# A two-block sequence model on one core: GpSimd's remainder of each weight block in four instructions of 256 columns instead of one of 1024

## The reference

```python
def swiglu(h, w_gate, w_up, w_down):
    return (jax.nn.silu(h @ w_gate) * (h @ w_up)) @ w_down

for i in range(DEPTH):
    x = x + 0.5 * swiglu(rmsnorm(x, ffn1_norm[i]), ffn1_w_gate[i], ffn1_w_up[i], ffn1_w_down[i])
    h = rmsnorm(x, mix_norm[i]) @ w_in[i]
    ...
    x = x + y @ w_out[i]
    x = x + 0.5 * swiglu(rmsnorm(x, ffn2_norm[i]), ffn2_w_gate[i], ffn2_w_up[i], ffn2_w_down[i])
```

## Time and profile before

| what | us |
|---|---|
| median of 3 runs | 3364.13 (3363.9 to 3365.0) |
| span of the profiled execution | 3360.4 |
| TensorE busy | 3228.2 (96%) |
| VectorE busy | 1812.3 (54%) |
| GpSimd busy | 1835.2 (55%) |
| ScalarE busy | 748.6 (22%) |

### The profile page before, as it was taken

How to read it: one execution, slowest core, us unless ns; L and a number is a source line. 1 busy time by engine, 2 the same in 40 slices (tenths; PEclk the granted TensorE clock), 3 DMA queues, 4 the chain that set the end, 5 groups by cost and what they waited for, 6 DMA issues and landing times.

```text
span 3360.4 us, 44069 instructions
## 1 busy us (share of the span) xinstructions
PE 3228.2 (96%) x14534; PEld 2578.4 (77%) x14534; DVE 1812.3 (54%) x1971; ACT 748.6 (22%) x1260; POOL 1835.2 (55%) x1026
## 2 busy tenths in 40 slices
PE   8999998899999999999889999999999999999998
PEld 6788875578888778876567888788777877888886
DVE  7661277663313765138754331586768886753312
ACT  2110126422201111014532220111122322222200
POOL 5556651066666656663036666644455455666665
PEclk9999999999999999999999999999999999999999
DMA  4222320022323322331012222322122222223322
GB/s 155 81 86 96 113 76 26 9 86 94 100 94 103 110 79 89 100 107 56 13 44 88 98 96 98 118 76 69 63 85 69 76 69 70 94 94 94 97 96 81
DMA packets 77430, 281.26 MB, mean 84 GB/s; under 512 B 9382, under 2 KB 9766, under 8 KB 76776
## 3 DMA queue, kind: packets, MB, share of 16 engines
q1 hardware_dynamic: 74016, 268.58, 24.5%
q10 hardware_dynamic: 3272, 10.79, 0.9%
HBM read 277.24 MB, written 2.10 MB: 83 GB/s over the span
## 4 chain that ended last, share of the span: by engine, by line
PE 79%; DVE 15%; issue 4%; ACT 2%; DVEq 0%; DMA 0%; ACTq 0%; SPq 0%
PE bank L505 24%; PE bank L510 23%; PE bank L509 23%; DVE short L1938 1%; PE bank L640 1%; PE bank L725 1%; PE bank L790 1%; DVE square_sum L1727 1%; DVE xbc L2276 1%; DVE y L1970 1%; DVE x_lo L1717 1%; DVE scaled L2114 1%; PE bank L799 1%; DVE att_qk L2212 0%; DVE reach L2369 0%
## 5 line engine op out<-in xcount | busy, mean ns | idle before, releaser
L451 POOL TENSOR_SCALAR w_hi<-raw 128x1024 fp32r<-128x1024 f32 x504 | 554.8, 1101 | 1451.4 <-PE bank L505 1443.0
L454 POOL TENSOR_TENSOR w_lo<-raw,w_hi 128x1024 fp32r<-128x1024 f32 x504 | 1267.5, 2515 | 42.0
L505 PE MATMUL bank<-x_hi,w_hi 128*128 128x512 f32 x2896 | 1151.3, 398 | 47.7 <-DVE x_lo L1717 21.6
L510 PE MATMUL bank<-x_hi,w_lo 128*128 128x512 f32 x2896 | 1134.6, 392 | 0.0
L509 PE MATMUL bank<-x_lo,w_hi 128*128 128x512 f32 x2896 | 1134.0, 392 | 0.0
L505 PEld LDWEIGHTS bank<-x_hi,w_hi 128*128 128x128 f32 x2896 | 547.8, 189 | 183.4 <-issue 66.4
L510 PEld LDWEIGHTS bank<-x_hi,w_lo 128*128 128x128 f32 x2896 | 547.6, 189 | 116.2
L509 PEld LDWEIGHTS bank<-x_lo,w_hi 128*128 128x128 f32 x2896 | 547.8, 189 | 114.5 <-issue 4.1
L505 PE MATMUL bank<-hidden_hi,w_hi 128*128 (+1 forms) x880 | 342.3, 389 | 0.0
L509 PE MATMUL bank<-hidden_lo,w_hi 128*128 (+1 forms) x880 | 342.3, 389 | 0.0
L510 PE MATMUL bank<-hidden_hi,w_lo 128*128 (+1 forms) x880 | 342.3, 389 | 0.0
(11 more groups left out here) (382 smaller groups left out, 3229.1 us busy)
## 6 DMA issues: line engine op xcount, KB each, us to landing
raw<-in_w SPq DMA_DIRECT2D x504, 512.0 KB, 3.6
dft<-in_dft ACTq DMA_DIRECT2D x2, 1536.0 KB, 6.6
out<-x SPq DMA_DIRECT2D x4, 512.0 KB, 2.6
mask<-in_mask ACTq DMA_DIRECT2D x1, 1536.0 KB, 7.2
x<-in_x SPq DMA_DIRECT2D x2, 512.0 KB, 5.9
x<-in_x SPq DMA_DIRECT2D x1, 1024.0 KB, 8.8
filt_cos<-in_dft_filter ACTq DMA_DIRECT2D x2, 512.0 KB, 6.5
filt_sin<-in_dft_filter ACTq DMA_DIRECT2D x2, 512.0 KB, 8.1
```

Of the source, the lines that this page charges most:

```text
L451: nc.gpsimd.tensor_scalar(w_hi[:, s % 2, :], raw[:, s, :], 1.0, 0.0, ALU.mult, ALU.add).then_inc(w_rounded, 1)
L454: nc.gpsimd.tensor_tensor(w_lo[:, s % 2, :], raw[:, s, :], w_hi[:, s % 2, :].bitcast(F32), ALU.subtract).then_inc(w_split, 1)
L505: first = nc.tensor.matmul(out, hi_w, hi, start=start, stop=False)
L510: return nc.tensor.matmul(out, lo_w, hi, start=False, stop=stop)
```

## The change

The subtraction that makes `w_lo` is issued as four instructions, each on 256 of the 1024 columns, one behind the other with no wait in between. The wait for `w_hi` stands in front of the first, and only the last raises `w_split`.

```diff
                 pool.wait_ge(w_rounded, n + 1)
-                nc.gpsimd.tensor_tensor(w_lo[:, s % 2, :], raw[:, s, :], w_hi[:, s % 2, :].bitcast(F32),
-                                        ALU.subtract).then_inc(w_split, 1)
+                for part in range(4):
+                    at = slice(part * 2 * P, (part + 1) * 2 * P)
+                    rest = nc.gpsimd.tensor_tensor(w_lo[:, s % 2, at], raw[:, s, at],
+                                                   w_hi[:, s % 2, at].bitcast(F32), ALU.subtract)
+                rest.then_inc(w_split, 1)
```

## The result

The changed kernel takes 3369.31 us (median of 20 runs, 3365.39 to 3373.33), the kernel before 3362.89 us in the same comparison (20 runs, 3359.66 to 3365.32). The ratio is 1.0021, with a 95% interval of 1.0014 to 1.0027: slower by 0.2%, some 6 us, where 0.7% faster had been forecast. It lies just inside the forecast's range, on the other side. The profiled execution took 3373.1 us with a span of 3371.0; the kernel before had 3360.4.

A forecast was written before the change was run, and what follows sets the result against it. TensorE, busy 96% of the span, was taken as the bound, with GpSimd hidden. Idle time -36, clock -8 and late remainders +13 gave -31 us, cut to -23: 3341 us, range 3316 to 3370.

The forecast's parts named there:

- 36 us of idle time: TensorE idle time saved by shorter VectorE waits, added up over stretches where the chain runs over VectorE: 36 us.
- step (4): TensorE's clock: half of ten dips to the lower level behind idle gaps taken as gone, 8 us saved.
- The rival in which the change does nothing: GpSimd keeps the port through all four quarters, so VectorE's long waits stay: 3366 us, chance 0.10.
- step (5): VectorE operations let in between quarters make remainders late for TensorE: 8 us before feed-forward inputs, 5 in filter stages, 13 together.
- The estimate of 0.82 us: Time of one 256-column quarter on a line through the skill's 2048-column figure and the trace's 1024: 3.3 us for four.
- The room: How much later GpSimd's remainder could end in an undisturbed block before TensorE missed it: about 1.3 us.
- the decision point: Two VectorE operations inside a remainder make it 1.35 us later, and TensorE, which had 1.3, begins to wait.
- The discount of a quarter: Only three quarters of the net -31 us counted, because TensorE's waits have other paths just behind: -23 us.
- GpSimd becomes the bound: In back-to-back weight blocks, quarters at 0.85 us with VectorE operations inserted make GpSimd slower than TensorE: 3394 us, chance 0.14.

The follow-up runs named there:

- the early start: Quarters kept, but TensorE starts a block after the first quarter and waits for the last only before the third tile; 3322.61 us against 3362.97 for the kernel before.

## Why the prediction failed

**Right: the mechanism and its gain.** A two-input VectorE operation waited for a whole GpSimd instruction, and it gets its turn between two that follow each other. The single place in the earlier trace rows told that correctly. The sum had 36 us of idle time and 8 us of clock on the gain side; with the price taken away by the early start, 40 us came back: 28.7 us of TensorE's idle time (132.2 to 103.5) and 12.0 of its busy time. The early start's mean granted clock is 0.989 in the profiled execution against 0.987; 0.002 of 3360 us is about 7 us, against the 8 of step (4). By stretch the sum was less good: the work of 457:501 gave 3.8 us of the forecast 6.0 with the early start and 3.5 in the change itself; one of its two gaps, 2.32 us for `x_lo`, hardly shrank. The rival in which the change does nothing fell with the maxima of L2212 and L1938, 1.93 and 1.50 us where below 1.9 was forecast.

**Wrong: step (5), the price.** It said 13 us: "about 1 us each" at eight strings, and 15 blocks by 0.33 us in the filter stages. The runs show 47 us (6 slower for the change, 40 faster for the early start). Set against the table of block starts, the strings and the filters, for which it had 8 and 5 us, cost 11.5 and 11.7 us. The other half, some 26 us in the plain feed-forward blocks and in the mixers, had no term at all. The sizes behind it:

- A quarter takes 0.70, not 0.66 us: the remainder is 0.43 us later where it is quiet, not 0.25. The estimate of 0.82 us that the figure in the Trainium skill, GPSIMD Engine Reference, section 3.1, gave was further off on the other side (3.3 us for four, where the trace has 2.83); its fixed part of 0.29 us is 0.15 here. (Drawn again, that line gives 0.30 and 0.83, which changes nothing.)
- The room was called 1.3 us. But TensorE's block begins 0.15 us after the last quarter's end (784.12 to 784.27). From TensorE's start that makes 0.59 + 1.05 + 0.09 + 2.40 + 0.15 = 4.28 us, so 1.17 us to spare, not 1.3.
- What two operations add was taken as 2 x 0.55 = 1.1 us and is less: 3.59 - 2.83 = 0.76 us in the feed-forward. So the remainder is 1.19 us later with two, not 1.35. This error went the other way.
- I looked for two operations inside one remainder only in the strings. The plainest feed-forward has them: L1755 and L1757, 110 times each. The timeline of the kernel before at 784 us shows them side by side. 1.19 us later against 1.17 to spare is just too late: the block's first matmul starts 0.02 us later and its second another 0.07, in every second block there. In the filters, the convolutions' taps, the second network and the strings three to five get in, and a block start loses 0.3 to 1.25 us.

The forecast had the decision point right, "with two inside, ... TensorE, which had 1.3, begins to wait", and then counted the places where it happens far too low. The discount of a quarter, for paths just behind, fits the idle time (28.7 of 36 us came back) but was not needed for the rest, which gave 12 instead of 8. The rival "GpSimd becomes the bound" was priced at 0.85 us per quarter; late blocks needed only 0.70. The net result, 6 us slower, is gain minus price of nearly the same size, and so nothing that one view of the trace shows. That it lies inside the forecast's range is luck: the range was drawn for a gain with a small price.

What stays open: how much of the 47 us is TensorE's clock. In the two profiled executions its mean hardly differs, 0.990 after and 0.989 with the early start, and the change, though slower, has a higher one than the kernel before (0.987). So it should be little, but no run held it fixed.

## What to carry to other kernels

When a hidden engine's long instruction is cut so that another engine may get in, both engines' times change: write down the hidden engine's whole cycle with the guests that it will now let in, including the signal to its consumer, and compare it with the consumer's cycle in the plainest and most repeated stage, not only where the gain is. A cut pays if the consumer can start on the first piece, as the runs with the early start show; without that, the coarser cut (two parts) won and the finest (eight) lost 5%. And a consumer that loses 0.1 us per block shows no wait at all, and one that loses 0.6 shows a shorter one: hold the starts of the same instructions in both traces against each other, not windows of the same times, which hold different work once one kernel is late.

## What was not expected of the hardware

A GpSimd subtraction of this kind, undisturbed, costs a fixed 0.15 us and 2.16 ns per column from start to start: 0.16 us for 6 columns, 0.42 for 128, 0.70 for 256, 1.25 for 512 and 2.36 for 1024 fit one line. And the turn is not strict. In one place a quarter that waited while two VectorE operations followed each other without a gap was passed over by both:

```profile
2175.38 2.24 POOL L456 TENSOR_TENSOR w_lo<-raw,w_hi 128x256 fp32r<-128x256 f32 x1
...
2175.75 0.67 DVE L2466 TENSOR_TENSOR turn<-turn,rstd 128x512 f32<-128x512 f32 x1
2176.35 0.67 DVE L2467 TENSOR_TENSOR turn<-turn,rstd 128x512 f32<-128x512 f32 x1
```

This quarter took 2.24 us instead of 0.74, while L2466 and L2467, each with two SBUF inputs, ran one behind the other.
